# Feed-forward's input projections: 19 pairs of blocks in seven products of quarters instead of eight

## The chip, the cores and the metric

One core of a Trainium2 chip runs one launch of this kernel. The metric is the time of the launch in microseconds on the device: 2751.25 as the median of 3 runs (2750.54 to 2753.55). Engine names are those of the profile: PE (TensorE matmul), PEld (its weight loads), ACT (ScalarE), DVE (VectorE), POOL (GpSimd), SP (SyncE, which issues the weights' transfers).

## The reference

Two transformer-like blocks over 512 tokens of width 1024, in float32. The change touches the feed-forward part of the first block, with `D_FF = 2816`:

```python
hf = rms_norm(x, g_pre_ffn)
f_gate, f_up = jnp.split(hf @ w_ffn_in, 2, axis=-1)     # 1024 -> 2 x 2816
f = (jax.nn.silu(f_gate) * f_up) @ w_ffn_out
return x + rms_norm(f, g_post_ffn)
```

## The kernel before

The kernel keeps activations transposed: features on the 128 partitions, the 512 tokens along the free dimension. Every float32 operand of a matmul is split in two rounded parts, high and low. ACT writes the high part (`act_unit`, L497), DVE subtracts it from the raw value for the low part (`low_unit`, L504), and a product is three matmuls: high by high, high by low, low by high (L553 to L555).

Weights come in pieces of 128 x 2048 over a ring of three buffers, each issued by SP once both parts of everything in the buffer's last piece are written. A piece holds two units of 1024 columns, and the split parts have three slots of a unit each, so ACT and DVE work at most three units ahead of PE.

The feed-forward stage works in two halves, j = 0 and 1, each of 11 pairs of blocks. A pair is one piece: a gate block and an up block of 128 features each, with a contraction over 8 tiles of 128. `pe_gemm` (L539) runs a block as 8 x 3 matmuls of 128 x 128 weights by 128 x 512 activations into one PSUM bank. ACT takes SiLU of the gate block into `sg` (L2059). DVE multiplies the up block by it into `px` (L2088), ACT and DVE split the product into `ffn_p` (L988, L993), and after 11 pairs `pe_out_gemm` multiplies by w_fo0, after the second 11 `pe_seam_gemm` by w_fo1. The first three blocks (two half-blocks of 256 tokens each, L690 to L692) belong to `pe_entry` of the stage before (merge), whose last activations come in by token quarters.

The order of the work is written out by hand: one function per engine (`pe_ffn` L2038, `act_ffn` L2047, `dve_ffn` L2072, `pool_ffn` L2097), each engine runs its list in that order and waits on semaphores named by events. `gemm_steps` (L512) sets where a unit's split stands among the drains. POOL has little to do here: it issues the transfers of the gains (L961) and multiplies by a gain at the end (L971).

## Time and profile before

| | |
|---|---|
| median of the runs | 2751.25 us |
| profiled execution | 2753.57 us, span 2751.9 us, granted clock 0.997 |
| PE busy | 2665.4 us, 97%, 21832 matmuls |
| DVE busy | 1464.0 us, 53% |
| ACT busy | 1216.2 us, 44% |
| POOL busy | 304.4 us, 11% |
| DMA | 227.92 MB, mean 83 GB/s |

The feed-forward blocks that the change rewrites run from 836.6 us to 1119.5 us of the span, with w_fo0 between them. Busy time of PE is the time from each matmul's start to its modelled end, and matmuls overlap: how fast they follow one another is to be read from their starts.

### The profile page before, as it was taken

Reading aid. Unit: us, or ns where it says so; the run is one execution under the profiler, and the core shown is the slowest. Engines: PE = TensorE matmul, PEld = TensorE weight load, DVE = VectorE, ACT = ScalarE, POOL = GpSimd, SP = SyncE. Lnnn points to the kernel's source line nnn. Section 1 sums busy time; section 2 is a strip of 40 time slices with the busy share of each in tenths; the row PEclk is TensorE's granted clock in tenths of the full one; section 3 lists DMA queues with packets and bytes.
Section 4 is the critical chain, followed back from the end, with each engine's and each line's share of the span. In section 5 each row is a group of like instructions: output and inputs, shape, how many; then the busy total and the mean of one; then the engine's idle time right before and its main releaser. Section 6 shows DMA issues by size and latency. Waiting matters only on the chain. (4 is left out here: it accounts for less than half of the span.)

```text
span 2751.9 us, 50708 instructions
## 1 busy us (share of the span) xinstructions
PE 2665.4 (97%) x21832; PEld 2127.8 (77%) x21832; DVE 1464.0 (53%) x2371; ACT 1216.2 (44%) x2081; POOL 304.4 (11%) x261
## 2 busy tenths in 40 slices
PE   8999999999999999999999999999888989999999
PEld 7887567788888888886488888887677766788887
DVE  3536874744353333444754243497678775652343
...
PEclk9999999999999999999999999999999999999999
...
GB/s 188 98 77 93 1 24 92 77 125 113 100 92 108 100 95 105 115 106 78 56 103 99 107 92 96 106 90 93 10 6 12 8 8 67 113 110 92 92 107 62
DMA packets 38718, 227.92 MB, mean 83 GB/s; under 512 B 4401, under 2 KB 8497, under 8 KB 14945
## 3 DMA queue, kind: packets, MB, share of 16 engines
...
## 5 line engine op out<-in xcount | busy, mean ns | idle before, releaser
L504 DVE TENSOR_TENSOR weights_lo<-ring,weights_hi 128x1024 fp32r<-128x1024 f32 x347 | 428.1, 1234 | 661.4 <-ACT weights_hi L497 656.0
L497 ACT ACTIVATE weights_hi<-ring 128x1024 fp32r<-128x1024 f32 x346 | 364.0, 1053 | 494.1 <-PE bank L729 280.7
L553 PE MATMUL bank<-h_hi,weights_hi 128*128 128x512 f32 x384 | 150.2, 391 | 0.0
L727 PE MATMUL bank<-weights_hi,mlp_p_hi 128*128 128x512 f32 x384 | 149.7, 390 | 0.0
L554 PE MATMUL bank<-h_lo,weights_hi 128*128 128x512 f32 x384 | 149.6, 390 | 0.0
L728 PE MATMUL bank<-weights_lo,mlp_p_hi 128*128 128x512 f32 x384 | 149.5, 389 | 0.0
L729 PE MATMUL bank<-weights_hi,mlp_p_lo 128*128 128x512 f32 x384 | 149.5, 389 | 0.0
L555 PE MATMUL bank<-h_hi,weights_lo 128*128 128x512 f32 x384 | 149.5, 389 | 0.0
L553 PE MATMUL bank<-mlp_h_hi,weights_hi 128*128 128x512 f32 x336 | 130.8, 389 | 0.0
L554 PE MATMUL bank<-mlp_h_lo,weights_hi 128*128 128x512 f32 x336 | 130.8, 389 | 0.0
L555 PE MATMUL bank<-mlp_h_hi,weights_lo 128*128 128x512 f32 x336 | 130.8, 389 | 0.0
L2570 DVE TENSOR_TENSOR mlp<-mlp 128x512 f32<-128x512 f32 x64 | 44.3, 692 | 115.1 <-ACT mlp L2528 115.1
L553 PE MATMUL bank<-ffn_h_hi,weights_hi 128*128 128x512 f32 x248 | 96.6, 389 | 0.0
L554 PE MATMUL bank<-ffn_h_lo,weights_hi 128*128 128x512 f32 x248 | 96.6, 389 | 0.0
L555 PE MATMUL bank<-ffn_h_hi,weights_lo 128*128 128x512 f32 x248 | 96.5, 389 | 0.0
L553 PEld LDWEIGHTS bank<-h_hi,weights_hi 128*128 128x128 f32 x384 | 72.1, 188 | 18.4 <-issue 3.6
L555 PEld LDWEIGHTS bank<-h_hi,weights_lo 128*128 128x128 f32 x384 | 72.1, 188 | 15.0
L729 PEld LDWEIGHTS bank<-weights_hi,mlp_p_lo 128*128 128x128 f32 x384 | 72.1, 188 | 15.0
L728 PEld LDWEIGHTS bank<-weights_lo,mlp_p_hi 128*128 128x128 f32 x384 | 72.1, 188 | 14.9
L554 PEld LDWEIGHTS bank<-h_lo,weights_hi 128*128 128x128 f32 x384 | 72.1, 188 | 14.8
L727 PEld LDWEIGHTS bank<-weights_hi,mlp_p_hi 128*128 128x128 f32 x384 | 72.1, 188 | 14.8
L1005 ACT ACTIVATE scan_low<-bank 128x512 f32<-128x512 f32 x80 | 43.4, 595 | 88.5 <-PE bank L2940 70.4
...
## 6 DMA issues: line engine op xcount, KB each, us to landing
ring<-in_w_m SPq DMA_DIRECT2D x64, 1024.0 KB, 4.8
ring<-in_w_mb SPq DMA_DIRECT2D x24, 1024.0 KB, 4.8
ring<-in_w_fi SPq DMA_DIRECT2D x22, 1024.0 KB, 4.8
ring<-in_w_fo SPq DMA_DIRECT2D x10, 1024.0 KB, 4.9
ring<-in_w_a SPq DMA_DIRECT2D x7, 1024.0 KB, 4.9
...
ring<-in_w_rg SPq DMA_DIRECT2D x5, 1024.0 KB, 4.9
ring<-in_w_v SPq DMA_DIRECT2D x4, 1024.0 KB, 10.8
```

Source lines behind the costliest of these rows:

```text
L497: act.e.activation(halves(g, s)[0], raw, ACT.Copy).then_inc(*act.up("act_unit_high", ("high", s)))
L504: lane.e.tensor_tensor(lo, raw, hi.bitcast(F32), ALU.subtract).then_inc(*lane.up(f"{lane.name}_unit_low", ("low", s)))
L553: pe.e.matmul(ps[:, :], hi, xh, start=k == 0, stop=False, skip_group_check=True)
L554: pe.e.matmul(ps[:, :], hi, xl, start=False, stop=False, skip_group_check=True)
L555: m = pe.e.matmul(ps[:, :], lo, xh, start=False, stop=k == kt - 1, skip_group_check=True)
L727: pe.e.matmul(ps[:, :], xh, hi, start=k == 0, stop=False, skip_group_check=True)
L728: pe.e.matmul(ps[:, :], xh, lo, start=False, stop=False, skip_group_check=True)
L729: m = pe.e.matmul(ps[:, :], xl, hi, start=False, stop=k == kt - 1, skip_group_check=True)
L1005: return lane.e.activation(dst, src, ACT.Copy).then_inc(*lane.up("act_drained", *events))
L2570: dve.e.tensor_tensor(x, q, q, ALU.mult).then_inc(*dve.up("dve_squared", ("squared", layer, j, i), ("relu_read", layer, j, i)))
```

## The change

The first three pairs of the first half stay as they are. The other 8 pairs of it and all 11 of the second are computed by Winograd's form of Strassen's scheme. A pair is a 256 x 1024 matrix A (gate rows over up rows) by a 1024 x 512 matrix B (the activations). Both are cut in quarters: A11 and A12 are the gate block's first and second four tiles of the contraction, A21 and A22 the up block's; B is cut by contraction (first index) and by 256 tokens (second index). Then

```
S3 = A11 - A21   S2 = A22 - S3   S1 = S2 + A11   S4 = A12 - S2
T1 = B12 - B11   T2 = B22 - T1   T3 = B22 - B12  T4 = B21 - T2
r = A11.B11      bank x: r + A12.B21 (gate, tokens 0 to 255)
bank y: S2.T2, then + S3.T3      u2 = r + S2.T2      u3 = r + S2.T2 + S3.T3
bank a: S1.T1, then + S4.B22     c22 = u3 + S1.T1    c12 = u2 + S1.T1 + S4.B22
bank b: A22.T4                   c21 = u3 + A22.T4
```

Each product is 4 x 3 matmuls of 128 x 128 by 128 x 256. The sums S are made for every pair by POOL from the raw float32 weights, in the ring's buffer and one extra tile `s2`. The sums T are made once: T1, T2 and T4 by DVE, T3 by POOL, from the parts of the activations, and split again; T3 takes B12's place once the last old block is read. The operand slots are now six halves of a unit. ACT splits five operands ahead of the product on PE and DVE four. ACT copies r out of its bank, DVE forms u3, c22, c21, u2 and c12, and the SiLU is taken in halves of 256 tokens. w_fo0 and w_fo1 keep their form.

```diff
+OPERANDS = ("A11", "S2", "S1", "A12", "S3", "A22")
+AHEAD = 4
+WINO = {"w_fi0": range(3, HFF), "w_fi1": range(HFF)}
...
+    F.T["T3"] = F.T["B12"]
...
+MOVING = {"A11": "B11", "S2": "T2", "S1": "T1", "A12": "B21", "A22": "T4", "S3": "T3", "S4": "B22"}
+BANK = {"A11": "x", "A12": "x", "S2": "y", "S3": "y", "S1": "a", "S4": "a", "A22": "b"}
...
+def operand_raw(g, name, p, op):
+    raw = g.slots[(PIECE0[name] + p) % RING]
+    return g.F.s2 if op == "S2" else raw[:, {"A11": 0, "S1": 0, "A12": 512, "S4": 512, "S3": 1024, "A22": 1536}[op]:][:, 0:512]
...
+def act_operand(g, act, name, n):
+    p, op = SEQ[name][n]
+    if op in ("A11", "A12", "A22"):
+        act.wait_ge(g.at("landed", PIECE0[name] + p))
+    else:
+        act.wait_ge(g.at("sum", name, p, op))
+    for event in FREED[(name, n)]:
+        act.wait_ge(g.at(*event))
+    act.e.activation(operand_halves(g, name, n)[0], operand_raw(g, name, p, op), ACT.Copy).then_inc(
+        *act.up("act_unit_high", ("high", (name, p, op))))
+def dve_operand(g, dve, name, n):
+    p, op = SEQ[name][n]
+    hi, lo = operand_halves(g, name, n)
+    dve.wait_ge(g.at("high", (name, p, op)))
+    dve.e.tensor_tensor(lo, operand_raw(g, name, p, op), hi.bitcast(F32), ALU.subtract).then_inc(
+        *dve.up("dve_unit_low", ("low", (name, p, op))))
...
+def pool_sum(g, pool, name, p, op):
+    def raw(q):
+        return operand_raw(g, name, p, q)
+    i = PIECE0[name] + p
+    pool.wait_ge(g.at("landed", i))
+    if op == "S3":
+        pool.e.tensor_tensor(raw("S3"), raw("A11"), raw("S3"), ALU.subtract).then_inc(*pool.up("pool_sum", ("sum", name, p, op)))
+        return
+    before = wino_before(name, p)
+    if op == "S2" and before:
+        pool.wait_ge(g.at("low", before + ("S2",)))
+        pool.wait_ge(g.at("sum", *before, "S4"))
+    pool.wait_ge(g.at("sum", name, p, "S3" if op == "S2" else "S2"))
+    if op == "S1":
+        pool.wait_ge(g.at("high", (name, p, "A11")))
+        pool.wait_ge(g.at("low", (name, p, "A11")))
+        pool.e.tensor_tensor(raw("S1"), g.F.s2, raw("A11"), ALU.add).then_inc(*pool.up("pool_sum", ("sum", name, p, op)))
+        return
+    if op == "S4":
+        pool.wait_ge(g.at("high", (name, p, "A12")))
+        pool.wait_ge(g.at("low", (name, p, "A12")))
+        pool.e.tensor_tensor(raw("S4"), raw("A12"), g.F.s2, ALU.subtract).then_inc(*pool.up("pool_sum", ("sum", name, p, op)))
+        return
+    pool.e.tensor_tensor(g.F.s2, raw("A22"), raw("S3"), ALU.subtract).then_inc(*pool.up("pool_sum", ("sum", name, p, op)))
...
+def pool_sums(g, pool, name):
+    for p in WINO[name]:
+        pool_sum(g, pool, name, p, "S3")
+        if p > WINO[name][0]:
+            pool_sum(g, pool, name, p - 1, "S4")
+        for op in ("S2", "S1"):
+            pool_sum(g, pool, name, p, op)
+    pool_sum(g, pool, name, WINO[name][-1], "S4")
...
+def pe_wino(g, pe, name):
+    F = g.F
+    last = WINO[name][-1]
+    for n, (p, op) in enumerate(SEQ[name]):
+        key, begun = (name, p, BANK[op]), op in ("A12", "S3", "S4")
+        ps = g.psum[g.bank_of[key]] if begun else bank(g, pe, key)
+        ps = ps[:, 0:256]
+        pe.wait_ge(g.at("high", (name, p, op)))
+        pe.wait_ge(g.at("low", (name, p, op)))
+        if MOVING[op] in ("T1", "T2", "T3", "T4"):
+            pe.wait_ge(g.at("turned_high", MOVING[op]))
+            pe.wait_ge(g.at("turned_low", MOVING[op]))
+        if begun:
+            pe.wait_ge(g.at({"A12": "r", "S3": "u2", "S4": "c22"}[op], name, p))
+        hi, lo = operand_halves(g, name, n)
+        xh, xl = F.T[MOVING[op]]
+        for k in range(4):
+            w = slice(k * P, k * P + P)
+            pe.e.matmul(ps, hi[:, w], xh[:, k, :], start=k == 0 and not begun, stop=False, skip_group_check=True)
+            pe.e.matmul(ps, hi[:, w], xl[:, k, :], start=False, stop=False, skip_group_check=True)
+            m = pe.e.matmul(ps, lo[:, w], xh[:, k, :], start=False, stop=k == 3, skip_group_check=True)
+        m.then_inc(*pe.up("pe_product", ("product", name, n), ("done", name, p, op)))
...
-    pe_gemm(g, pe, "w_fi0", NB, range(3, 2 * HFF), part_of(F.hs), lambda nb, k: ())
+    pe_gemm(g, pe, "w_fi0", NB, range(3, 6), part_of(F.hs), lambda nb, k: ())
+    pe_wino(g, pe, "w_fi0")
     pe_out_gemm(g, pe, "w_fo0", HFF, lambda k: cols(F.prs, k), lambda k: split_events(("ffn", 0, k)))
     pe.mark("ffn_read", 0)
-    pe_gemm(g, pe, "w_fi1", NB, range(2 * HFF), part_of(F.hs), lambda nb, k: ())
+    pe_wino(g, pe, "w_fi1")
...
+def act_ffn_wino(g, act, j):
+    F, name = g.F, f"w_fi{j}"
+    for n, (p, op) in enumerate(SEQ[name] + [(None, None)] * 3):
+        before = SEQ[name][n - 1] if 0 < n <= len(SEQ[name]) else (None, None)
+        if before[1] == "A11":
+            q = before[0]
+            ps = wino_bank(g, act, name, q, "A11")
+            if q - 2 >= WINO[name][0]:
+                act.wait_ge(g.at("u3", name, q - 2))
+            elif j:
+                act.wait_ge(g.at("u3", "w_fi0", HFF - 1))
+            act.e.activation(F.r[q % 2], ps, ACT.Copy).then_inc(*act.up("act_first", ("r", name, q)))
+        if before[1] == "A12":
+            q = before[0]
+            act_silu(g, act, j, q, wino_bank(g, act, name, q, "A12"), slice(0, 256), ("silu_first", j, q), ("drained", (name, q, "x")))
+        if n < len(SEQ[name]):
+            split_ahead(g, act, name, n)
+        if n == len(SEQ[name]):
+            act_unit(g, act, SPLIT0[name] + 2 * HFF + 2)
+        if n >= 2 and n < len(SEQ[name]) + 2 and SEQ[name][n - 2][1] == "S4":
+            q = SEQ[name][n - 2][0]
+            act.wait_ge(g.at("c12", name, q))
+            act_silu(g, act, j, q, F.sg[buffer_of(j, q)][:, 256:512], slice(256, 512), ("silu", j, q))
+        if n >= 3 and SEQ[name][n - 3][1] == "S4":
+            act_ffn_high(g, act, j, SEQ[name][n - 3][0])
...
+    u = SPLIT0["w_fi0"]
+    for nb in range(3):
+        for i in (2 * nb, 2 * nb + 1):
+            if i % 2 == 0:
+                act_silu(g, act, 0, nb, filled(g, act, ("w_fi0", i))[:, :], slice(0, S), ("silu", 0, nb), ("drained", ("w_fi0", i)))
             else:
-                act.wait_ge(g.at("product", j, nb))
-                if j:
-                    act.wait_ge(g.at("ffn_read", 0))
-                high_part(g, act, ("ffn", j, nb), F.px[nb % 2], cols(F.prs, nb))
-        if j == 0:
-            first_part_copies(g, act, F.t)
+                act_ffn_high(g, act, 0, nb)
+            if i == 0:
+                act_turn_high(g, act, "T1")
+            if i == 1:
+                act_turn_high(g, act, "T2", ("unit_read", u))
+            if i == 3:
+                act_turn_high(g, act, "T4", ("unit_read", u + 1))
+            split_next(g, act, u + 3 + i)
+    act_turn_high(g, act, "T3", ("filled", ("w_fi0", 5)))
+    act_ffn_wino(g, act, 0)
+    first_part_copies(g, act, F.t)
+    act_ffn_wino(g, act, 1)
...
+def dve_turn(g, dve, name, first, second, third=None, events=()):
+    F = g.F
+    raw = F.raws[name]
+    for event in events:
+        dve.wait_ge(g.at(*event))
+    (a, b), ops = first, (ALU.subtract, ALU.add, ALU.subtract)
+    for q, op in zip((b, second, third), ops):
+        if q is None:
+            continue
+        dve.e.tensor_tensor(raw, a, q, op).then_inc(*dve.up("dve_turned", ("turned_raw", name)))
+        dve.wait_ge(dve.newest)
+        a = raw
...
+def dve_ffn_product(g, dve, j, nb):
+    sg, x = g.F.sg[buffer_of(j, nb)], g.F.px[buffer_of(j, nb)]
+    dve.wait_ge(g.at("silu", j, nb))
+    dve.wait_ge(g.at("silu_first", j, nb))
+    dve.wait_ge(g.at("c22", f"w_fi{j}", nb))
+    dve.e.tensor_tensor(x, x, sg, ALU.mult).then_inc(*dve.up("dve_drained", ("product_split", j, nb), ("silu_read", j, nb)))
...
+def dve_ffn_wino(g, dve, j):
+    F, name = g.F, f"w_fi{j}"
+    for n in range(len(SEQ[name]) + 4):
+        before = SEQ[name][n - 1] if 0 < n <= len(SEQ[name]) else (None, None)
+        q = before[0]
+        if before[1] == "S3":
+            ps = wino_bank(g, dve, name, q, "S3")
+            dve.wait_ge(g.at("r", name, q))
+            if wino_before(name, q):
+                dve.wait_ge(g.at("c21", *wino_before(name, q)))
+            dve.e.tensor_tensor(F.u3, ps, F.r[q % 2], ALU.add).then_inc(
+                *dve.up("dve_wino", ("u3", name, q), ("drained", (name, q, "y"))))
+            dve_ffn_free(g, dve, j, q)
+            ps = wino_bank(g, dve, name, q, "S1")
+            dve.wait_ge(g.at("u3", name, q))
+            dve.e.tensor_tensor(F.px[buffer_of(j, q)][:, 256:512], ps, F.u3, ALU.add).then_inc(*dve.up("dve_wino", ("c22", name, q)))
+        if before[1] == "A22":
+            ps = wino_bank(g, dve, name, q, "A22")
+            dve.e.tensor_tensor(F.px[buffer_of(j, q)][:, 0:256], ps, F.u3, ALU.add).then_inc(
+                *dve.up("dve_wino", ("c21", name, q), ("drained", (name, q, "b"))))
+        if before[1] == "S2":
+            ps = wino_bank(g, dve, name, q, "S2")
+            dve.wait_ge(g.at("r", name, q))
+            dve.e.tensor_tensor(F.u2[q % 2], ps, F.r[q % 2], ALU.add).then_inc(*dve.up("dve_wino", ("u2", name, q)))
+        if before[1] == "S4":
+            ps = wino_bank(g, dve, name, q, "S4")
+            if ffn_before(j, q):
+                dve.wait_ge(g.at("silu_read", *ffn_before(j, q)))
+            dve.wait_ge(g.at("u2", name, q))
+            dve.e.tensor_tensor(F.sg[buffer_of(j, q)][:, 256:512], ps, F.u2[q % 2], ALU.add).then_inc(
+                *dve.up("dve_wino", ("c12", name, q), ("drained", (name, q, "a"))))
+        if n < len(SEQ[name]):
+            split_ahead(g, dve, name, n)
+        if n == len(SEQ[name]):
+            low_unit(g, dve, SPLIT0[name] + 2 * HFF + 2)
+        if 3 <= n < len(SEQ[name]) + 3 and SEQ[name][n - 3][1] == "S4":
+            dve_ffn_product(g, dve, j, SEQ[name][n - 3][0])
+        if 4 <= n and SEQ[name][n - 4][1] == "S4":
+            dve_ffn_low(g, dve, j, SEQ[name][n - 4][0])
...
+    u, T = SPLIT0["w_fi0"], {name: [q.bitcast(F32) for q in pair] for name, pair in F.T.items()}
+    for q in range(QT):
+        for c in range(2):
+            for event in split_events((F.t_first, q, c)):
+                dve.wait_ge(g.at(*event))
+    dve_turn(g, dve, "T1", (T["B12"][0], T["B11"][0]), T["B12"][1], T["B11"][1])
+    split_next(g, dve, u + 3)
+    dve_turn(g, dve, "T2", (T["B22"][0], F.raws["T1"]), T["B22"][1])
+    for nb in range(3):
+        x = F.px[buffer_of(0, nb)]
+        if nb == 1:
+            dve_turn(g, dve, "T4", (T["B21"][0], F.raws["T2"]), T["B21"][1], events=(("unit_read", u),))
+        ps = filled(g, dve, ("w_fi0", 2 * nb + 1))
+        dve.wait_ge(g.at("silu", 0, nb))
+        dve_ffn_free(g, dve, 0, nb)
+        dve.e.tensor_tensor(x, ps[:, :], F.sg[buffer_of(0, nb)], ALU.mult).then_inc(
+            *dve.up("dve_drained", ("drained", ("w_fi0", 2 * nb + 1)), ("product_split", 0, nb), ("silu_read", 0, nb)))
+        if nb == 1:
+            dve_turn_low(g, dve, "T1")
+            dve_turn_low(g, dve, "T2")
+        dve_ffn_low(g, dve, 0, nb)
+        if nb < 2:
+            split_next(g, dve, u + 4 + 2 * nb)
+            split_next(g, dve, u + 5 + 2 * nb)
+        else:
+            split_next(g, dve, u + 8)
+        if nb == 1:
+            dve_turn_low(g, dve, "T4")
+    dve_turn_low(g, dve, "T3")
+    dve_ffn_wino(g, dve, 0)
+    first_part_copies(g, dve, F.t)
+    dve_ffn_wino(g, dve, 1)
...
+    hi, lo = ({name: F.T[name][j].bitcast(F32) for name in ("B12", "B22")} for j in range(2))
+    for q in range(QT):
+        for c in range(2):
+            for event in split_events((F.t_first, q, c)):
+                pool.wait_ge(g.at(*event))
+    a = hi["B22"]
+    for q, op in ((hi["B12"], ALU.subtract), (lo["B22"], ALU.add), (lo["B12"], ALU.subtract)):
+        pool.e.tensor_tensor(F.raw3, a, q, op).then_inc(*pool.up("pool_turned", ("turned_raw", "T3")))
+        pool.wait_ge(pool.newest)
+        a = F.raw3
+    pool.wait_ge(g.at("unit_read", SPLIT0["w_fi0"] + 1))
+    pool_sums(g, pool, "w_fi0")
+    pool_sums(g, pool, "w_fi1")
```

Not shown are the tables that give each operand its half slot and the event that frees it (`slot_tables`; in the second half three half slots are left out, one in each of pairs 1 to 3), the wrapper `split_next` that lets the loops of other stages split operands or units, and SP's wait for all seven operands of a piece.

## Rows read from the trace of the kernel before

**Rows 1.** The page: busy time, share and count; granted clock in tenths by 40 slices.
```profile
PE 2665.4 (97%) x21832; PEld 2127.8 (77%) x21832; DVE 1464.0 (53%) x2371; ACT 1216.2 (44%) x2081; POOL 304.4 (11%) x261
...
PEclk9999999999999999999999999999999999999999
```
**Rows 2.** Groups, 836.3 to 940: busy us, mean ns | idle before, releaser.
```profile
L553 PE MATMUL bank<-ffn_h_hi,weights_hi 128*128 128x512 f32 x120 | 46.7, 389 | 0.0
...
L504 DVE TENSOR_TENSOR weights_lo<-ring,weights_hi 128x1024 fp32r<-128x1024 f32 x20 | 24.5, 1226 | 33.8 <-ACT weights_hi L497 33.8
```
**Rows 3.** Lines 553 and 727, 836 to 1200: ns min/median/max, first and last start.
```profile
L553 PE MATMUL bank<-ffn_h_hi,weights_hi x248: 388/389/396, 836.6 to 1118.8; 128*128 128x512 f32 x124
...
L727 PE MATMUL banks<-weights_hi,ffn_p_hi x22: 388/389/390, 939.9 to 967.8; 128*128 128x512 f32 x22
```
**Rows 4.** PE in order of time: start us, duration us; a half-block's first matmuls.
```profile
827.79 0.28 PE L692 MATMUL bank<-ffn_h_hi,weights_lo 128*128 128x256 f32 x1
827.91 0.28 PE L690 MATMUL bank<-ffn_h_hi,entry_hi 128*128 128x256 f32 x1
...
830.79 0.28 PE L690 MATMUL banks<-ffn_h_hi,entry_hi 128*128 128x256 f32 x1
```
**Rows 5.** DVE in order of time, 1940 to 1949: three splits of 512.
```profile
1940.68 1.87 DVE L993 TENSOR_TENSOR mix_small_lo<-x,mix_small_hi 128x512 fp32r<-128x512 f32 x3
...
1946.22 2.34 DVE L993 TENSOR_TENSOR mix_small_lo<-x,mix_small_hi 128x512 fp32r<-128x512 f32 x3 [0.45 <-ACT mix_small_hi L988]
```
**Rows 6.** POOL and DVE in order of time, 1959.5 to 1960.5.
```profile
1959.40 1.28 POOL L3315 TENSOR_TENSOR scan_b<-scan_a,scan_head 128x512 f32<-128x512 f32 x1 [12.59 <-DVE scan_a L3274]
1959.55 0.43 DVE L3274 TENSOR_TENSOR scan_a<-bank,scan_c 128x256 f32<-128x256 f32 x1
...
1959.89 0.41 DVE L3274 TENSOR_TENSOR x<-bank,scan_c 128x256 f32<-128x256 f32 x1
1960.22 0.41 DVE L3274 TENSOR_TENSOR scan_a<-bank,scan_c 128x256 f32<-128x256 f32 x1
```
**Rows 7.** DVE in order of time, 1148 to 1158.
```profile
1147.95 1.23 DVE L504 TENSOR_TENSOR weights_lo<-ring,weights_hi 128x1024 fp32r<-128x1024 f32 x1 [3.02 <-ACT weights_hi L497]
...
1153.46 2.11 DVE L504 TENSOR_TENSOR weights_lo<-ring,weights_hi 128x1024 fp32r<-128x1024 f32 x1 [1.89 <-ACT weights_hi L497]
1155.49 2.31 DVE L504 TENSOR_TENSOR entry_lo<-ring,entry_hi 128x1024 fp32r<-128x1024 f32 x1
```
**Rows 8.** POOL in order of time: beside the rows of 7, and of 5.
```profile
1153.19 1.29 POOL L971 TENSOR_TENSOR ffn<-ffn 128x512 f32<-128x512 f32 x1
...
1154.44 2.27 POOL L971 TENSOR_TENSOR ffn<-ffn 128x512 f32<-128x512 f32 x1
...
1944.65 2.16 POOL L3106 TENSOR_TENSOR ring<-rwkv,scan_head 128x512 f32<-128x512 f32 x1
```
**Rows 9.** ACT in order of time, 824 to 858.
```profile
832.35 0.60 ACT L2059 ACTIVATE ffn<-bank 128x512 f32<-128x512 f32 x1
832.85 1.05 ACT L497 ACTIVATE weights_hi<-ring 128x1024 fp32r<-128x1024 f32 x1
835.89 0.63 ACT L988 ACTIVATE ffn_p_hi<-ffn 128x512 fp32r<-128x512 f32 x1 [1.99 <-DVE ffn L2088]
836.43 1.04 ACT L497 ACTIVATE weights_hi<-ring 128x1024 fp32r<-128x1024 f32 x1
```
**Rows 10.** Groups by shape, ACT: a copy of 256 columns out of PSUM.
```profile
L1005 ACT ACTIVATE scan_c<-bank 128x256 f32<-128x256 f32 x16 | 5.2, 378 | 0.0
```
**Rows 11.** Start of the stage: DVE, POOL; and POOL's operations of 1024.
```profile
834.03 1.23 DVE L504 TENSOR_TENSOR weights_lo<-ring,weights_hi 128x1024 fp32r<-128x1024 f32 x1 [7.24 <-ACT weights_hi L497]
...
828.62 1.05 POOL L961 DMA_DIRECT2D ffn<-in_gains  x2 [142.85 <-PE bank L692]
...
L504 POOL TENSOR_TENSOR weights_lo<-ring,weights_hi x3: 2353/2357/2381, 227.4 to 232.1; 128x1024 fp32r<-128x1024 f32 x3
```
**Rows 12.** Transfers, 815 to 960: KB each, median us to landing.
```profile
ring<-in_w_fi SPq DMA_DIRECT2D x7, 1024.0 KB, 4.9
```

More of the change, by code:

```diff
@@ L307, in memory @@
     ffn_out, ffn_gains = a.take3(QT, D), a.take(2 * D)
+    F.raw3 = three(ffn_out[:, 0, :], S // 2)
+    F.T, F.raws, at = {}, {"T3": F.raw3}, W0 + 2 * NB * S + 2 * HFF * S + a.top
+    for name in ("T1", "T2", "T4"):
+        F.T[name] = [three(area(f"ffn_{name}_{part}", at + j * 1024, 1024, F32R), S // 2) for j, part in ((1, "hi"), (0, "lo"))]
+        F.raws[name] = three(area(f"ffn_{name}_raw", at, 1024), S // 2)
+        at += 2048
+    quarter = [three(p, S) for p in F.hs]
+    F.T.update({f"B{r + 1}{c + 1}": [p[:, 4 * r:4 * r + 4, 256 * c:256 * c + 256] for p in quarter] for r in range(2) for c in range(2)})
+    F.T["T3"] = F.T["B12"]
+    a = Shelf("ffn_parts", at, END - at)
+    F.s2 = a.take(512)
+    F.r, F.u2 = ([a.take(256) for _ in range(2)] for _ in range(2))
+    F.u3 = a.take(256)
     A = Core()
@@ L494, in act_unit @@
             act.wait_ge(g.at(*event))
-    elif before_in_ring(s) >= 0:
-        act.wait_ge(g.at("unit_read", before_in_ring(s)))
+    for event in () if s in ENTRY else FREED.get(s, ()):
+        act.wait_ge(g.at(*event))
     act.e.activation(halves(g, s)[0], raw, ACT.Copy).then_inc(*act.up("act_unit_high", ("high", s)))
@@ L977, in first_part_copies @@
         if what == "unit":
[L978 removed]
+            split_next(g, lane, i)
         elif turns(i[1]) == lane.name:
@@ new lines, in piece_split @@
+def piece_split(i):
+    if not wino_piece(i):
+        return [(part, s) for s in range(len(SPLIT)) if SPLIT[s][1] == i for part in ("high", "low")]
+    name, p = wino_piece(i)
+    return [(part, (name, p, op)) for op in OPERANDS + ("S4",) for part in ("high", "low")]
+def act_operand(g, act, name, n):
[5 more added lines that the diff above has]
+    for event in FREED[(name, n)]:
+        act.wait_ge(g.at(*event))
+    act.e.activation(operand_halves(g, name, n)[0], operand_raw(g, name, p, op), ACT.Copy).then_inc(
+        *act.up("act_unit_high", ("high", (name, p, op))))
@@ new lines, in dve_operand, with split_next @@
+def dve_operand(g, dve, name, n):
[4 more added lines that the diff above has]
+        *dve.up("dve_unit_low", ("low", (name, p, op))))
+def split_next(g, lane, s):
+    name, piece, _ = SPLIT[s]
+    first, split = (act_unit, act_operand) if lane.name == "act" else (low_unit, dve_operand)
+    if not wino_piece(piece):
+        first(g, lane, s)
+        return
+    n = 2 * (s - SPLIT0[name] - 2 * WINO[name][0])
+    for i in range(n, min(n + 2, AHEAD + (lane.name == "act"))):
+        split(g, lane, name, i)
@@ L3996, in sp_program @@
         if i >= RING:
-            if i - RING in units:
-                for s in units[i - RING]:
-                    sp.wait_ge(g.at("high", s))
-                    sp.wait_ge(g.at("low", s))
-            else:
+            if PIECES[i - RING][0] in RAW:
                 sp.wait_ge(g.at("raw_read", i - RING))
+            for event in () if PIECES[i - RING][0] in RAW else piece_split(i - RING):
+                sp.wait_ge(g.at(*event))
         if i == ro:
```

124 lines of the change are left out of this document (84 added, 40 removed).

## The prediction

 Busy time of pipelined matmuls proves little, so next the groups of the first feed-forward stretch: no idle time before its matmuls, and DVE's splits there wait only for the high parts from ACT [rows 2]. The order of time gives TensorE's pace. From the first 512-column matmul after the entry blocks (836.6) to the first of w_fo0 (939.9) lie 19 blocks of 24 [rows 3]: 103.3 / 456 = 0.2265 us each. The stage is TensorE's queue and nothing else; DVE spends 24.5 us of 103 on 20 splits [rows 2]. A change there counts through TensorE's issue, or through a wait that does not exist yet.
>
> **What TensorE saves.** A pair of blocks is now 48 matmuls of 512 columns, 48 x 0.2265 = 10.87 us. After it is seven products of 12 matmuls of 256 columns. The entry blocks already issue that shape: 24 of them, 827.91 to 830.79 [rows 4], 0.1200 each, so 84 x 0.1200 = 10.08 us. Their weight loads hide too, or the pace would not be 0.12. 19 pairs x 0.79 = 15.0 us less, if everything else keeps up. That is the whole gain; matmuls fall by an eighth in columns but rise from 912 to 1596 in number.
>
> The Trainium skill ("TensorE: Matmul & The Clock Gate", Back-to-back issue gap) gives a sustained 81 ns at 128 columns and 131 ns at 512. By that an estimate of 98 ns at 256 makes a pair 8.2 us against 6.3 us, a loss of 1.9 us a pair, 36 us in all. This trace does not agree: 227 and 120 ns [rows 3, 4]; the rows decide.
>
> **What the other engines get, per pair.** ACT: 7 high parts of 512 and the product's high part, 8 x about 0.53 (0.63 long, the next begins 0.54 after it [rows 9]); three operations of 256, 0.38 each [rows 10]: 5.4 us. It keeps up. DMA: one piece per pair as before, 4.9 us to land [rows 12], issued when the last of the seven operands is split, some five products before TensorE is through with the next pair: hidden.
>
> DVE: nine operations of 512 with two SBUF inputs (7 low parts, the SiLU product, its low part) at a pace of 0.59 ((1.87 - 0.69) / 2 [rows 5]) = 5.3 us; five sums of 256 with one PSUM input at a pace of 0.335 [rows 6] = 1.7, plus 0.15 where one waits for the other's result: 7.1 us. Alone that fits in 10.08.
>
> GpSimd: four sums of 512, 1.28 each [rows 6], 5.1 us. Alone that fits too. Together they do not. A DVE split that takes 1.23 us alone took 2.11 and 2.31 beside GpSimd's sums; it ended 1.09 us after GpSimd's sum did (1154.48 to 1155.57; 1156.71 to 1157.80), and the fourth sum, 1.29 alone, took 2.27 and ended 1.14 after DVE's operation [rows 7, 8]. The two take turns, one whole operation each. Of three DVE operations of 512 begun 0.6 us before the end of a sum (1944.65 + 2.16 = 1946.81) the last ended at 1948.56, three paces after it [rows 5, 8]. But DVE operations with a PSUM input kept 0.41 to 0.43 us beside a sum of 1.28 [rows 6]. So each sum holds SBUF-only DVE work for up to 1.13 us, PSUM-fed work not at all.
>
> The Trainium skill ("SBUF — State Buffer", SBUF: two separate sides) calls the shared port pair an exclusive lock for the whole instruction, against DVE operations with two SBUF inputs. It speaks against this change, and the trace agrees in kind; by whole durations it would be 9 x 0.69 + 4 x 1.28 = 11.3 us a pair. The rows show start-up outside the lock (0.56 and 1.13 held), 9.6 us, and the walk below is what decides.
>
> **Walk through one pair,** from the end of the low part of A12 (t = 0); DVE splits four operands ahead, so it is not held by TensorE when it is behind. S4 of the pair before waited for this low part; its event comes after DVE has taken the next low part (S3), to 0.59. S4's sum holds the port to 1.73; u2 runs beside it, the low of A22 waits to 2.29. S2's sum 2.29 to 3.43, c12 beside it, low of A11 to 3.99. S2's high part (ACT, 0.63) is there at 4.2; S1's sum got in first, 4.12 to 5.26; low of S2 5.82; sum S3 to 6.96; low of S4 7.52; product 8.11; u3, c22 8.93; low of S1 9.52; low of the product 10.11; c21 10.45; low of A12 11.04. DVE's cycle is 7.1 + 3.9 = **11.04 us, over TensorE's 10.08 and over the old 10.87.** Bounds: below, every sum falls beside PSUM-fed or idle DVE time: 10.08; above, none does and each handover costs its whole start-up, 7.1 + 4 x 1.28 = 12.2. I take 11.04, the walk by the handovers of rows 7 and 8, which is nearest to how these queues are filled.
>
> **The start of the stage.** Now nothing runs on DVE for 7.2 us, to 834.0 [rows 11]. Added: T1, T2, T4 (7 operations of 1024) and four low parts on DVE, four high parts on ACT, and T3 (3 operations of 1024, 2.36 each [rows 11]) on GpSimd, behind its gain DMAs at 828.6. T1 (3 x 1.09) is interleaved with T3: 828.2 to about 834.0, where it alone would end at 831.8. Behind it on ACT, T1's high part and then the high of block 3's unit, to 836.1 instead of 833.9; its low at 837.3; block 3, due at 836.55, starts 0.85 late. Queued behind on DVE: the last third of T3 (to 839.5), T2 with the first sums between, to 842.9, then product 0; on ACT product 0's high part, T2's high part, the high of block 4's unit, 846.3. Its low is 847.4. Block 4 was ready to start at 842.9: **4.6 us of stall.** At the third product in the new form A12 waits for the copy r, which stands on ACT behind the last old product, operand 4, T3 and operand 5: 2.0 us, and u2 0.5. TensorE starts its fifth product at 866.9 instead of 858.6: 8 us late. Bounds: 0 (nothing is taken away there that could gain) to 12 if T3 also comes ahead of block 3's low part.
>
> **Sum.** First half: from 866.9 DVE's cycle runs 7 times, 77.3, to 944.2; the last pair's c22, without the operands of a next one but with a unit of w_fo0 (1.2), 3.5 more, then S4's 12 matmuls 1.45: w_fo0 begins at 949.2 instead of 939.9: +9.3. Second half: its first operands are split while w_fo0 still runs, so DVE starts level: u2 at 3.1, ten cycles 110.4, tail 3.5 + 1.45 = 118.5 against 22 x 5.44 = 119.6: -1.1. Together +8.2. The products' extra bank waits fall within DVE's lead and cost 0; without that lead they'd be in the cycle already counted. w_fo0 and w_fo1 keep their form, and their last k is read 27 us after the stage ends, so the later product is covered. The profiled execution took 2753.57 (span 2751.9 and 1.7 around it), 2.3 above the median: 2761.8 for it, **2759 us** for the median.
>
> **Rivals.**
> - TensorE stays the bound, since sums fall into DVE's gaps. For it: DVE's 7.1 leaves 3.0 us idle in 10.08, and with 1.7 of PSUM-fed work that just holds 4 x 1.13 = 4.5. Against: it needs a perfect fit, and in rows 7 and 8 none occurs. Start stall 4 to 8: -15.0 + 6 = -9, 2742. Chance 0.22.
> - A slower loop: the sums wait for low parts (S1 for A11, S4 for A12), ACT waits for the sums, DVE for ACT. The place is the low of S2: its sum, 1.13, then 0.63 of ACT, has 4.0 us of DVE work as cover and needs 4.2. It decides from a cover of under 4 us. With 0.4 lost at two such places a cycle is 11.8, 17 cycles x 0.76 = 13 more: 2772. Chance 0.17.
> - A tie, cycle near 10.5, the saving eaten by the start: 17 x 0.54 = 9 under the forecast: 2750. Chance 0.06.
> - It does not do what it says: 84 matmuls of 256 columns slower than 0.12 because of waits at each product. At the entry four waits stand before a block, and the pace across the seam at 827.91 stays 0.12 [rows 4]. Within the forecast's range.
>
> **Numbers.** Forecast 0.55, with a cycle of 10.8 to 11.3 and a start of 5 to 10: 2753 to 2767. About 0.2% (5.5 us) is what can be told from no change. Faster: the first rival, 0.22. Same: the tie and a third of the forecast, 0.24. Slower: the rest, 0.54. The range for 8 in 10 reaches into both rivals: 2740 to 2775.
>
> **What would show it.** DVE near 100% busy, not 80%, in both stretches, its low parts of 512 with a mean of 0.9 or more instead of 0.69 and forms of 1.8; GpSimd's sums with a mean of 1.5 or more; PSUM-fed sums of 256 still 0.42. TensorE idle before the products, released by DVE, 1 us a pair; 256-column matmuls 0.12 apart inside a product. At 843 a gap of 4 to 5 us before block 4. It is wrong if low parts stay at 0.69 beside the sums, or if product follows product with no gap.

## The result, and the profile after

| | kernel before (with three more runs than above) | changed kernel |
|---|---|---|
| median (lowest to highest), us | 2751.89 (2748.57 to 2759.45) | 2764.15 (2762.99 to 2766.55) |
| runs | 6 | 6 |
| profiled execution, span, us | 2753.57, 2751.9 | 2765.13, 2763.4 |

The ratio is 1.0041, 95% interval [1.0029, 1.0052]: slower by 8 to 14 us, where 7.8 had been forecast (2759 in 2740 to 2775).

The page of the changed kernel, against [rows 1]: TensorE issues 684 matmuls more and is busy 6.5 us less, DVE is busy 147 us more and GpSimd 134 us more.

```profile
PE 2658.9 (96%) x22516; PEld 2152.9 (78%) x22516; DVE 1610.5 (58%) x2572; ACT 1264.4 (46%) x2218; POOL 438.3 (16%) x340
```

Busy times by stretch, once within each half of the stage. The columns are: the stretch, its length in us, busy us and count of PE, PEld, DVE, ACT and POOL, granted clock, DMA share, GB/s. DVE is busy for 97.5% of the first stretch and 97.8% of the second, at a full clock: it sets the pace, and TensorE does not.

```profile
881.90:937.60 55.70, 52.86 (x437) 52.33 (x436) 54.33 (x73) 27.27 (x56) 32.13 (x19) 1.00 0.27 94
1018.60:1106.60 88.00, 82.83 (x681) 81.78 (x681) 86.05 (x109) 43.15 (x89) 53.02 (x32) 1.00 0.27 91
```

One DVE cycle, which is DVE's work for one pair of blocks, in order of time, from u3 (L2384) to the next u3, 893.12 to 904.38 (start us, duration us). L2133 is the low part of an operand, L1047 the product's, L2366 the SiLU product; L2384, L2389, L2392, L2397 and L2403 are u3, c22, c21, u2 and c12, fed from PSUM. GpSimd's rows of the same time stand behind it.

```profile
893.12 0.41 DVE L2384 TENSOR_TENSOR ffn_parts<-banks,ffn_parts 128x256 f32<-128x256 f32 x1
893.64 0.42 DVE L2389 TENSOR_TENSOR ffn<-bank,ffn_parts 128x256 f32<-128x256 f32 x1
893.98 0.68 DVE L2133 TENSOR_TENSOR weights_lo<-ring,weights_hi 128x512 fp32r<-128x512 f32 x1
894.58 0.69 DVE L1047 TENSOR_TENSOR ffn_p_lo<-ffn,ffn_p_hi 128x512 fp32r<-128x512 f32 x1
895.18 0.42 DVE L2392 TENSOR_TENSOR ffn<-bank,ffn_parts 128x256 f32<-128x256 f32 x1
895.51 1.29 DVE L2133 TENSOR_TENSOR weights_lo<-ring,weights_hi 128x512 fp32r<-128x512 f32 x2
896.72 0.42 DVE L2397 TENSOR_TENSOR ffn_parts<-bank,ffn_parts 128x256 f32<-128x256 f32 x1
897.05 1.45 DVE L2133 TENSOR_TENSOR weights_lo<-ring,weights_hi 128x512 fp32r<-128x512 f32 x1
898.43 0.41 DVE L2403 TENSOR_TENSOR ffn<-bank,ffn_parts 128x256 f32<-128x256 f32 x1
898.76 1.45 DVE L2133 TENSOR_TENSOR weights_lo<-ring,weights_hi 128x512 fp32r<-128x512 f32 x1
900.36 0.69 DVE L2133 TENSOR_TENSOR weights_lo<-ffn_parts,weights_hi 128x512 fp32r<-128x512 f32 x1
900.97 1.79 DVE L2133 TENSOR_TENSOR weights_lo<-ring,weights_hi 128x512 fp32r<-128x512 f32 x1
902.68 1.78 DVE L2366 TENSOR_TENSOR ffn<-ffn 128x512 f32<-128x512 f32 x1
904.38 0.41 DVE L2384 TENSOR_TENSOR ffn_parts<-bank,ffn_parts 128x256 f32<-128x256 f32 x1
```

```profile
896.34 1.61 POOL L2183 TENSOR_TENSOR ring<-ring,ffn_parts 128x512 f32<-128x512 f32 x1 [3.69 <-ACT weights_hi L2125]
898.03 1.63 POOL L2185 TENSOR_TENSOR ffn_parts<-ring 128x512 f32<-128x512 f32 x1
900.38 1.83 POOL L2178 TENSOR_TENSOR ring<-ffn_parts,ring 128x512 f32<-128x512 f32 x1 [0.72 <-ACT weights_hi L2125]
902.17 1.74 POOL L2168 TENSOR_TENSOR ring<-ring 128x512 f32<-128x512 f32 x1
```

Four GpSimd sums, and beside each one DVE operation of 512 takes 1.45 to 1.79 instead of 0.69, as in [rows 7, 8]. Each of the four ends 0.55 behind the end of its sum (897.95 and 898.50, 899.66 and 900.21, 902.21 and 902.76, 903.91 and 904.46): it was held until the sum was nearly done. c12 at 898.43 runs inside a sum and keeps 0.41, as in [rows 6].

TensorE's waits in the stage, 836 to 1140 (waited for: us, times, longest us):

```profile
PE bank L2224 <- DVE ffn L2389: 9.6, 11, 1.0
PE bank L607 <- DVE weights_lo L558: 4.0, 2, 3.3
PE banks L2224 <- ACT ffn_parts L2290: 1.4, 1, 1.4
PE banks L2224 <- DVE ffn_parts L2397: 0.6, 1, 0.6
```

The start, in order of time. On DVE T1's last two operations and block 3's low part:

```profile
829.59 7.16 DVE L2348 TENSOR_TENSOR ffn_T_raw<-ffn_T_raw,ffn_h_lo 128x1024 f32<-128x1024 f32 x2
838.89 1.23 DVE L558 TENSOR_TENSOR weights_lo<-ring,weights_hi 128x1024 fp32r<-128x1024 f32 x1 [2.14 <-ACT weights_hi L551]
```

On GpSimd T3's last two operations:

```profile
832.40 6.57 POOL L2465 TENSOR_TENSOR ffn<-ffn,ffn_h_lo 128x1024 f32<-128x1024 f32 x2
```

On TensorE block 3's first matmul:

```profile
840.26 0.77 PE L607 MATMUL bank<-ffn_h_hi,weights_hi 128*128 128x512 f32 x1 [3.34 <-DVE weights_lo L558]
```

Behind that gap TensorE's granted clock was low, by the same columns as above:

```profile
842.00:844.00 2.00, 2.00 (x6) 1.52 (x6) 1.97 (x2) 0.00 (x0) 1.47 (x1) 0.50 0.95 385
846.00:848.00 2.00, 2.00 (x11) 1.65 (x10) 0.79 (x2) 2.00 (x3) 0.00 (x0) 1.00 0.00 0
```

Where the 11.5 us between the two spans arose, by the start of the same work in both traces: w_fo0 begins at 947.9 instead of 939.9 (+8.0); the second half takes 178.3 instead of 179.6 (-1.3), so the stage gives +6.8 with rounding. The rest, +4.8, comes 850 us later, in the RWKV scan (a later part of the kernel, of many small matmuls), whose code is the same (between 1978 and 2373 of the kernel before).

### The profile page after: what moved, and what is told of

Same layout as the page of the kernel before. It is cut to its first block and busy times, and to the rows that moved or that the text cites. A ratio compares the mean times of both kernels' runs of the same rounds, so it can differ in the third digit from the quotient of the medians.

```text
span 2763.4 us, 52772 instructions
## 1 busy us (share of the span) xinstructions
PE 2658.9 (96%) x22516; PEld 2152.9 (78%) x22516; DVE 1610.5 (58%) x2572; ACT 1264.4 (46%) x2218; POOL 438.3 (16%) x340
## 5 line engine op out<-in xcount | busy, mean ns | idle before, releaser
L558 DVE TENSOR_TENSOR weights_lo<-ring,weights_hi 128x1024 fp32r<-128x1024 f32 x309 | 381.5, 1235 | 571.7 <-ACT weights_hi L551 566.3
L551 ACT ACTIVATE weights_hi<-ring 128x1024 fp32r<-128x1024 f32 x308 | 324.0, 1054 | 482.3 <-PE bank L783 266.2
L2133 DVE TENSOR_TENSOR weights_lo<-ring,weights_hi 128x512 fp32r<-128x512 f32 x114 | 119.4, 1061 | 12.7 <-ACT weights_hi L2125 12.7
L2125 ACT ACTIVATE weights_hi<-ring 128x512 fp32r<-128x512 f32 x114 | 68.2, 622 | 42.5 <-POOL ring L2178 15.8
L1059 ACT ACTIVATE scan_low<-bank 128x512 f32<-128x512 f32 x80 | 43.4, 595 | 90.7 <-PE bank L3310 71.0
L608 PEld LDWEIGHTS bank<-h_lo,weights_hi 128*128 128x128 f32 x384 | 72.1, 188 | 14.8
L2898 ACT ACTIVATE mlp<-bank 128x512 f32<-128x512 f32 x46 | 27.4, 596 | 104.2 <-PE bank L609 104.2
```

Source lines behind the costliest of these rows:

```text
L551: act.e.activation(halves(g, s)[0], raw, ACT.Copy).then_inc(*act.up("act_unit_high", ("high", s)))
L558: lane.e.tensor_tensor(lo, raw, hi.bitcast(F32), ALU.subtract).then_inc(*lane.up(f"{lane.name}_unit_low", ("low", s)))
L608: pe.e.matmul(ps[:, :], hi, xl, start=False, stop=False, skip_group_check=True)
L2125: act.e.activation(operand_halves(g, name, n)[0], operand_raw(g, name, p, op), ACT.Copy).then_inc(*act.up("act_unit_high", ("high", (name, ...
L2133: dve.e.tensor_tensor(lo, operand_raw(g, name, p, op), hi.bitcast(F32), ALU.subtract).then_inc(*dve.up("dve_unit_low", ("low", (name, p, o ...
```

## The experiments

All ratios are against the kernel before on the same chip. "Offset at 1126" is by how much the first work behind the stage is later than in the trace of before; "in the scan" is by how much that offset grows between 1978 and 2373 of before. Each offset comes from one profiled execution, and single executions differ: the kernel before took 2748.07 to 2760.46 in the 26 runs beside e1, and the profiled execution of e6, 2741.46, lies 3.8 under e6's median.

| kernel | median, us | ratio, interval | DVE's cycle, us | offset at 1126 | in the scan |
|---|---|---|---|---|---|
| changed kernel | 2764.15 | 1.0041 [1.0029, 1.0052] | 11.25 | +6.8 | +4.8 |
| e1, sums of 8 columns | 2750.33 | 0.9979 [0.997, 0.9988] | 10.08 | -9.7 | +5.6 |
| e2, more work in each sum | 2815.77 | 1.0227 [1.0194, 1.026] | 14.06 | +58.1 | +4.3 |
| e3, T3 later | 2761.62 | 1.0033 [1.0023, 1.0043] | 11.25 | +6.7 | +2.1 |
| e5, sums on DVE | 2752.44 | 0.9994 [0.9985, 1.0003] | 10.08 | -4.1 | +4.5 |
| e10, new start only | 2759.08 | 1.0022 [1.0013, 1.003] | 11.25 | +1.3 | +1.8 |
| e6, sums on DVE, new start | 2745.24 | 0.9968 [0.9958, 0.9978] | 10.08 | -13.5 | +2.6 |
| e8, e6 with first u2 and r earlier | 2743.18 | 0.9959 [0.9948, 0.9971] | 10.08 | -15.5 | +2.9 |
| e7, before with sums on GpSimd | 2753.55 | 0.9997 [0.9986, 1.0008] | | -0.2 | -0.1 |
| e4, before with 30 matmuls more | 2762.82 | 1.0029 [1.0017, 1.0041] | | +6.4 | +1.5 |
| e9, before with 684 small matmuls | 2898.65 | 1.0532 [1.0516, 1.0549] | | +145.0 | -1.7 |
| e11, before with 342 | 2824.84 | one run | | +72.3 | +0.6 |

### Are the sums on GpSimd what makes DVE's cycle 11.25?

**e1** cuts every sum to 8 columns and takes A22 for the operand S2, so it leaves the sums out and its result is another one. Every wait, split, product and drain stays, and so does their order.

```diff
     def raw(q):
-        return operand_raw(g, name, p, q)
+        return operand_raw(g, name, p, q)[:, 0:8]
```

> The changed kernel with GpSimd's quarter sums cut to 8 of 512 columns, and the operand S2 read from A22 (the sums are left out of the computation; all waits, splits, products and drains stay). Theory (GpSimd's sums and DVE's operations with two SBUF inputs take turns, and that makes DVE's cycle 11.25 us a pair): low parts fall from a mean of 1.01 to 0.69 us, the cycle from 11.25 to TensorE's 10.08, 17 cycles x 1.17 = 20 us less than the changed kernel: 2744. Rival (DVE's own 14 operations and their waits for banks and high parts make the cycle, whatever GpSimd does): cycle stays above 11, 2764.

The cycle is 10.08 from the first on, low parts have a mean of 683 ns, and none of the 9.6 us of waiting for c22 is left. Groups on DVE in 881.9 to 937.6 (busy us, mean ns | idle before), of the changed kernel and then of e1:

```profile
L2133 DVE TENSOR_TENSOR weights_lo<-ring,weights_hi 128x512 fp32r<-128x512 f32 x30 | 33.3, 1123 | 0.0
L2366 DVE TENSOR_TENSOR ffn<-ffn 128x512 f32<-128x512 f32 x6 | 9.6, 1595 | 0.0
```

```profile
L2133 DVE TENSOR_TENSOR weights_lo<-ring,weights_hi 128x512 fp32r<-128x512 f32 x36 | 23.8, 683 | 2.4 <-ACT weights_hi L2125 2.4
L2366 DVE TENSOR_TENSOR ffn<-ffn 128x512 f32<-128x512 f32 x6 | 4.1, 685 | 0.0
```

By the traces 16.5 us of the stage are the columns of the sums. The median came out 6 us above the 2744 expected. The 20 us had been reckoned with 17 waits for c22, and the changed kernel has 11, so 3.5 of the 6 are missing in the stage already; another 1.4 are lost between 1126 and 1978, and 0.8 more than in the changed kernel in the scan.

**e2** puts another operation of 400 columns ahead of each sum, on GpSimd.

```diff
+    def twice(out, x, y, alu):
+        pool.e.tensor_tensor(g.F.junk, x[:, 0:400], y[:, 0:400], alu).then_inc(*pool.up("pool_junk"))
+        pool.wait_ge(pool.newest)
+        return pool.e.tensor_tensor(out, x, y, alu)
```

> The changed kernel with a second operation of 400 columns on GpSimd ahead of each quarter sum, into an unused tile (output is the reference's). Turn-taking: each holds DVE's SBUF-only work for about 0.9 us (400/512 of the sum's 1.13), four a pair on top of a cycle of 11.25: 14.8, over 17 cycles 61 us more than the changed kernel, 2825. If instead the sums cost only what their results' lateness costs, GpSimd's queue (4 x 2.25 = 9 us) still fits in the cycle and the time stays near 2764.

Cycle 14.06, 2.8 more for four operations more, and 29.9 us of waiting for c22 in 14 places. The time rises much as expected (2816 for 2825), but not for the reason given. Low parts from the ring keep their mean (1124 ns, 1123 in the changed kernel). What is new is 11.9 us in 55.7, 3.0 in each cycle, in which DVE stands idle before the low part of S2:

```profile
L2134 DVE TENSOR_TENSOR weights_lo<-ffn_parts,weights_hi 128x512 fp32r<-128x512 f32 x4 | 3.9, 985 | 11.9 <-ACT weights_hi L2126 11.9
```

DVE is busy for 78% of that stretch (43.4 of 55.7), not 98%, and GpSimd for 45.0. The extra work makes GpSimd's sums late, ACT's high part of S2 waits for its sum and DVE for the high part: the loop that was the second rival of the prediction, and the alternative in e2's expectation, which had put it at nothing. So e2 doesn't show what four more turns at the port cost.

**e5** keeps the scheme and every matmul and gives the sums to DVE, each behind the low part that frees its place; T3 stays on GpSimd.

```diff
     dve.e.tensor_tensor(lo, operand_raw(g, name, p, op), hi, ALU.subtract).then_inc(
         *dve.up("dve_unit_low", ("low", (name, p, op))))
+    dve_sum_after(g, dve, name, n)
...
-    pool_sums(g, pool, "w_fi0")
-    pool_sums(g, pool, "w_fi1")
```

> The changed kernel with the four quarter sums a pair on DVE, each behind the low part of another operand; GpSimd keeps T3 alone. Output is the reference's. Theory (turn-taking): DVE's cycle is 13 operations of 512 x 0.59 + 1.7 + 0.15 = 9.5 us, under TensorE's 10.08: 20 us less than the changed kernel, 2744, with low parts at 0.69. Rival (DVE is bound by its own work, 98% busy at 11.25 us): 2.4 us more work a pair, cycle 13.6, 2764 + 17 x 2.4 = 2805.

DVE has four operations more a pair and is faster for it: 13 of 512 at 0.60 and the rest fit in 10.08, while nine with the four on GpSimd do not. In time it fell short as e1 did, 2752 for the 2744 expected: the stage gave 10.9 us (+6.8 to -4.1), not 20, since TensorE keeps waits of 3.3, 2.2 and 0.6 us at the start. TensorE never waits within a product loop:

```profile
881.90:937.60 55.70, 55.70 (x466) 55.70 (x465) 53.08 (x100) 31.23 (x60) 0.00 (x0) 1.00 0.32 112
```

**e7** is the reverse: the kernel before, with four subtractions of 512 a pair on unused tiles on GpSimd.

```diff
+        for nb in range(0 if j else 3, HFF):
+            for k in range(4):
+                if k % 2 == 0:
+                    pool.wait_ge(g.at("high", SPLIT0[f"w_fi{j}"] + 2 * nb + k // 2))
+                pool.wait_ge(pool.newest)
+                pool.e.tensor_tensor(junk[1], junk[0], junk[1], ALU.subtract).then_inc(*pool.up("pool_junk"))
```

> The kernel before with four GpSimd subtractions of 512 columns for each of the 19 pairs, on unused tiles, set off by the pair's high parts; the products keep their old form. Turn-taking with room on DVE: its splits of 1024 stretch from 1.23 to up to 2.4 us, but DVE has 3.3 us of work in 10.87, so TensorE waits for nothing and the time is that of the kernel before within 0.2%. If the sums cost by themselves wherever they run, 19 x 1.2 = 22 us more.

It costs nothing. DVE is busy 20.2 of 55.7 us there and TensorE has no wait in the stage. The sums alone are harmless. DVE's splits kept their 1226 ns, though up to 2.4 had been expected, while GpSimd's operations took 1.8: here GpSimd was the one that was held, as both are set off by the same high part. What a held split would cost a DVE with time to spare is therefore not shown.

### The start

**e3** holds T3 until block 3's low part is made.

```diff
     a = hi["B22"]
+    pool.wait_ge(g.at("low", SPLIT0["w_fi0"] + 3))
```

> The changed kernel with GpSimd's three T3 operations held back until block 3's low part is written. Theory (T3 beside T1 makes the 3.6 us gap before block 3, and the gap the low clock behind it): block 3 on time, the granted clock stays 1.00 there, block 4 waits 2 to 3 us instead of 1.0 as T2 and T3 now take turns; 3 to 4 us less than the changed kernel, 2760. Rival (the gap is ACT's and DVE's own load): gap stays, 2764.

Block 3 is on time, as expected, but the gain of 3 to 4 us is not there: the offset at 1126 is +6.7 for +6.8. The gap has moved to block 4, one wait of 4.7 us at 847.3 in the place of two with 4.0, and the low clock with it (granted 0.50 from 848 to 852).

```profile
PE bank L607 <- DVE weights_lo L558: 4.7, 1, 4.7
```

**e6** is e5 with T3 on DVE behind block 3's product and what the first blocks need put ahead of the T parts. DVE's new order, in short; ACT's changes with it.

```diff
     dve_turn(g, dve, "T1", ...)
     dve_turn(g, dve, "T2", ...)
+    split_next(g, dve, u + 3)
+    dve_first_product(g, dve, 0)
+    dve_turn(g, dve, "T4", ...)
+    dve_ffn_low(g, dve, 0, 0)
+    split_next(g, dve, u + 4)
+    split_next(g, dve, u + 5)
+    dve_turn_low(g, dve, "T1")
+    dve_turn_low(g, dve, "T2")
+    dve_first_product(g, dve, 1)
+    dve_turn(g, dve, "T3", ...)
...
```

> e5 with the start of the stage reordered: T3 on DVE too, behind block 3's product instead of beside T1; high and low parts of the units that blocks 3, 4 and 5 need go ahead of T1's, T2's and T4's. Output is the reference's. Theory: the 3.6 us gap before block 3, its low clock (10 matmuls 0.43 apart instead of 0.23, 2.0 us) and 1.0 before block 4 go, 1 to 3 us stay at the third and fourth product: 5 us less than e5, 2739. Rival (DVE is now too full at the start, 28 us of work in 30): no better than e5, 2744.

Of the start's losses one wait of 1.4 us is left, and the clock stays at 1.00. e5 and e6 differ by 9.4 us at 1126. The median is 6 above the 2739 expected, as e5, from which it was reckoned, was 8 above its own.

**e10** is the fourth corner: the new start with the sums on GpSimd (the diff is against e6).

```diff
-    dve_sum_after(g, dve, name, n)
...
-    dve_first_sums(g, dve, "w_fi0")
...
+    pool_sums(g, pool, "w_fi0")
+    pool_sums(g, pool, "w_fi1")
```

> The fourth corner of two factors: the sums stay on GpSimd as in the changed kernel, the start is the reordered one (T3 on DVE after block 3's product, its first operands earlier). If the two losses are separate, the start as in e6 (one gap of under 2 us, first of w_fo0 about 7 x (11.25 - 10.08) = 8.2 after e6's 942.0: 950 is then too much by nothing else) and a cycle of 11.25: 2.2 us behind the kernel before when w_fo1 begins, 3 to 5 more in the scan: 2757 to 2759, ratio 1.002. Rival: the slow cycle came from the late start, which put the sums into an unlucky order; then the cycle is below 10.8 here and the ratio 0.998 or less.

The cycle is 11.25 again, so it does not come from a late start. Two factors, each with and without the other, in percent of the time: the sums off GpSimd save 0.47 (changed kernel to e5) and 0.54 (e10 to e6), the start 0.19 and 0.26. Within the intervals they add up. In the stage alone, by the traces at 1126, the sums are worth 10.9 and 14.8 us and the start 5.5 and 9.4: together some 4 us more than one by one.

**e8** forms the first u2 and the first r ahead of what stood before them.

```diff
     F, name = g.F, f"w_fi{j}"
+    if not j:
+        dve_u2(g, dve, name, WINO[name][0])
...
     act_turn_high(g, act, "T3", ("filled", ("w_fi0", 5)))
     split_next(g, act, u + 8)
+    act_r(g, act, "w_fi0", WINO["w_fi0"][0])
```

> e6 with the first u2 on DVE ahead of the fifth operand's low part, and the first copy r on ACT ahead of the last operand's high part (output is the reference's). e6's only gap left in the stage is 1.4 us at the fifth product, behind that u2: it goes, the stage ends 15 us before the old one's, 1.4 us less than e6, ratio 0.996.

No wait of TensorE is left from 836 to 1140. This version beats the kernel before by 0.3 to 0.5% and the changed one by 0.8%.

### The 4.8 us in the scan

**e4** is the kernel before with 30 matmuls of 512 ahead of w_fi1, each starting the bank anew.

```diff
+            for _ in range(30 if name == "w_fi1" and n == 0 else 0):
+                pe.e.matmul(ps[:, :], hi, xh, start=True, stop=False, skip_group_check=True)
```

> The kernel before with the first matmul of the second half's first block issued 30 times more (each restarts the bank, so nothing else changes), 30 x 0.2265 = 6.8 us of delay where the changed kernel is 6.6 us late. Question: where the other 4.8 us of the changed kernel come from, which its trace gains between 2000 and 2330 us, far behind the change. Theory A (what lies behind a delay is simply later): 2751.9 + 6.8 = 2758.7. Theory B (the stretch of small matmuls meets more low-clock stretches when it begins 7 us later): 2763 to 2764, with its trace 11 to 12 us late at 2330.

6.8 us behind the place, as 30 x 0.2265, of which 6.4 are left at 1126 against the trace of before, since e4's was 0.4 ahead; then 1.6 more near 1278, where the granted clock falls in e4 and not in the kernel before (0.79 from 1276 to 1284 of e4), and 1.5 in the scan. Less than the changed kernel loses there, yet not nothing: between the two theories.

**e9** and **e11** do the same with 684 and 342 matmuls of 32 columns.

```diff
+            for _ in range(684 if name == "w_fi1" and n == 0 else 0):
+                pe.e.matmul(ps[:, 0:32], hi, xh[:, 0:32], start=True, stop=False, skip_group_check=True)
```

> The kernel before with 684 more TensorE matmuls of 32 columns (as many more matmuls as the change has), all ahead of the first matmul of w_fi1's first block, each starting the bank anew; the result stays. They delay what follows by an amount that the trace gives (684 times 0.03 to 0.12). Theory A (TensorE's instruction supply in the scan stalls at places that hang on how many instructions it has issued): behind the delay, 2 to 6 us more are lost between 1980 and 2375 of the kernel before, as in all seven kernels that issue 684 more, with issue gaps at what was 2071 to 2073 and 2169 to 2172. Theory B (the loss hangs on the new code or on what the time is): under 1 us more, gaps where the kernel before has them (2026, 2035, 2260, 2265).

> As e9 with 342. Theory A: the gaps stand at a third set of places, and the drift within the scan is another number than e9's, anywhere from -2 to 6 us. Theory B: under 1 us, gaps as in the kernel before.

Theory A had given e9 a loss of 2 to 6 us in the scan. With the same number of matmuls as the changed kernel, e9 gained 1.7, and e11 lost 0.6. What holds of the theory: the waits that the profile puts down to "issue" do move. TensorE's in the scan, of the kernel before, the changed one and e9:

```profile
PE bank L2902 <- issue: 6.9, 9, 1.8
...
PE bank L2940 <- issue: 2.0, 1, 2.0
...
PE banks L2902 <- issue: 1.5, 1, 1.5
```

```profile
PE bank L3272 <- issue: 7.6, 10, 1.8
...
PE bank L3794 <- ACT scan_c L3836: 2.2, 2, 1.9
...
PE banks L3272 <- issue: 1.8, 1, 1.8
```

```profile
PE bank L2904 <- issue: 8.5, 10, 1.7
...
PE banks L2880 <- issue: 1.7, 2, 1.4
```

Their sum is 9.4 to 10.4 us in each; their places differ. And the places hang on TensorE's own instructions, as far as one execution of e11 shows it: e11, whose only edit is on TensorE, has its three longest before the operations at which the changed kernel has its own (2079.99, 2178.62 and 2318.20 there; 2074, 2168 and 2309 on the clock of the kernel before, which has none above 0.9 us at them). Two of e11's:

```profile
2142.77 0.34 PE L2904 MATMUL bank<-scan_low,scan_low 64*64 64x64 f32 x8 [1.51 <-issue]
2379.15 0.35 PE L2904 MATMUL bank<-scan_low,scan_low 64*64 64x64 f32 x9 [1.75 <-issue]
```

In the changed kernel one wait for ACT grew from 0.3 to 2.2. ACT waits there for DVE, and DVE for the port. Of the kernel before, and then of the changed one:

```profile
2097.25 0.68 DVE L3480 TENSOR_TENSOR scan_c<-scan_c 128x512 f32<-128x512 f32 x1
2097.31 2.85 POOL L3302 TENSOR_TENSOR bonus_lo<-scan_head,bonus_hi 128x1024 fp32r<-128x1024 f32 x1
```

```profile
2105.67 2.35 POOL L3672 TENSOR_TENSOR bonus_lo<-scan_head,bonus_hi 128x1024 fp32r<-128x1024 f32 x1
2105.80 2.77 DVE L3850 TENSOR_TENSOR scan_c<-scan_c 128x512 f32<-128x512 f32 x1
```

The same two operations meet. Before, DVE's begins 0.06 us ahead and takes 0.68; after the change GpSimd's begins 0.13 ahead, and DVE's takes 2.77 and holds up the chain: 1.9 of the 4.8 us. So it is in e1, e2, e3, e5, e8 and e10; in e6, and in e4, e7, e9 and e11, DVE's is ahead.

The clock differs too: granted 0.99 in the scan of before, 0.98 in that of the changed kernel, 1.00 in e9 and e11. In the traces that is 10.2, 13.7 and 3.4 us at the low level (1.2 GHz). At half a us lost for each, the most that half the clock can cost, it is an estimate of +1.7 us for the changed kernel and -3.4 for e9 and e11, which thus hides a loss in these two.

All eight kernels with the change's code lost 1.8 to 5.6 us in the scan, the four built on the old code -1.7 to +1.5. With the meeting and the clock's estimate taken off, it is 0.8 to 2.7 for the eight and -1.9 to 4.0 for the four, e11 at the upper end: no clear difference is left that goes with the new code on ACT and DVE. What decides where TensorE's waits fall, and with them who comes first at such a meeting, stays open.

## Why the prediction was right, and where it was not

**TensorE's pace** held: 256-column matmuls follow at 0.12 also across products (893.67, 893.79, ... 895.71), and e1, e5, e6 run at 10.08 a pair. The estimate of 98 ns from the figures of the Trainium skill ("TensorE: Matmul & The Clock Gate", Back-to-back issue gap), and with it 8.2 us a pair, is not borne out.

**DVE's cycle**, the step that decided the sign, was 11.04 in the walk and is 11.25. By the rows above, the four held operations take 1.38, 1.60, 1.71 and 1.70 to the next start instead of 0.60: 3.99 longer, where 3.9 had been predicted; 0.2 of it is the wait for the high part of S2, named below. The other 7.27 were given as 7.1. The order was nearly as walked: u2 and c12 beside the sums of S4 and S2, and a low part behind each of them; only the low part of S2 (900.36) got in ahead of the sum of S1, so that the sums of S1 and S3 held the low part after it and the product. Of the bounds, 10.08 is what e1 runs at; no run shows 12.2. The Trainium skill ("SBUF — State Buffer", SBUF: two separate sides) says that the two engines hold the port exclusively; the rows bear it out, held for less than an instruction's whole length: a held DVE operation ends 0.55 behind the sum and takes 0.69 alone. The sum by whole durations, 11.3, came nearer to 11.25 than the walk, but by chance: it leaves out the 1.7 of PSUM-fed work, and in the cycle above only two of its five operations run beside a sum. GpSimd's sums got slower too (1.61 to 1.83 for 1.28), which cost next to nothing here.

**TensorE's wait** is up to 1.2 us a pair at c22 over the pace, near the 0.96 forecast, but 11 times, not 17: the first cycles of each half use up DVE's lead, and the first half loses 4.3 us there instead of 6.7 (7 x 0.96).

**The start** was nearly right in its sum, by luck, and wrong in its parts. Predicted: 0.85 before block 3, 4.6 before block 4, 2.0 for r and 0.5 for u2, 8.0 together. Measured, by how much the matmul behind each wait is later than the pace would have it: 3.5, 0.8, 1.5 and 0.7, and a term the sum did not have: 13 matmuls at the low clock, 0.39 to 0.57 apart instead of 0.23, 2.7 us in all. That makes 9.2. The failed step is "T1 is interleaved with T3 ... to about 834.0". T3's operations got in twice, not once: T1's last two took 7.16 us for 2.3, and T1 ended at 836.75.

**Sum of the stage**: +9.3 - 1.1 = +8.2 predicted, +8.0 - 1.3 = +6.8 measured, rounded and with 0.2 by which the two traces differed ahead of it. The errors had opposite signs: 1.2 too little for the start, 2.4 too much for TensorE's waits in the first half. That the sum came so near is in part luck.

**What the forecast lacked** is the scan: 4.8 of the 11.5 us, 1.9 of them from one more meeting at the port. The forecast took what lies behind the stage to be merely later. The time came within the range since it was wide enough, not because that was seen.

**Rivals.** TensorE as the bound (0.22): not so; DVE's 3 us of idle time in 10.08 did not hold four sums of 1.13; the full cycles take 11.24 to 11.35. The slower loop by the low of S2: there is an idle 0.15 before it in the cycle above (900.21 to 900.36), so its cover of 4.0 against 4.2 was as tight as reckoned. It cost 0.2 a cycle (1.60 for 1.38 with the same duration of 1.45), not 0.8. In e2 it decides the cycle.
